# Rounded products for the projections of latent attention, and part of the output product moved into the last decoding sequence

## The chip, the cores and the metric

The kernel runs on one core of one Trainium2 chip. The time is the device time of one execution in microseconds (us). TensorE (PE) multiplies out of the on-chip memory into eight PSUM banks; VectorE (DVE) and ScalarE (ACT) empty these banks and prepare operands; GpSimd (POOL) does elementwise work; SyncE (SP) issues the transfers. The engines run side by side and wait for each other on semaphores.

## The reference, cut to what matters

Two layers of a decoder: the first mixes tokens by multi-head latent attention, the second by a recurrence (RWKV-7); each is followed by a feed-forward part (FFN). The change touches the first layer's attention alone. T = 1072 tokens: 16 meta tokens, 1024 of the prompt, and 8 sequences that are being decoded with 4 tokens each, which look back on 2048 cached tokens in pages of 128.

```python
a = h @ w_qkv_a
c_q = rmsnorm(a[..., :Q_LORA], q_a_norm)                    # 384 wide
c_kv = rmsnorm(a[..., Q_LORA:Q_LORA + KV_LORA], kv_a_norm)  # 256 wide
k_pe = rope(a[..., Q_LORA + KV_LORA:], pos)                 # 64 wide
q = (c_q @ w_q_b).reshape(B, T, 8, 128 + 64)
w_uk = w_kv_b.reshape(256, 8, 128 + 128)[..., :128]
...
hp = hp + o @ w_o      # o: attention output of all 8 heads, 1024 wide
hs = hs + o_sample @ w_o
```

## The kernel before

Everything is float32 and lies transposed: features on the 128 partitions, tokens along the row, in three pieces of 384, 384 and 304 tokens (`PIECES`). PE writes two rings of four PSUM banks: ring A is emptied by ACT, ring V by DVE. `Fill.bank` waits until the bank four fills ago was drained. A matmul on float32 operands is recorded as two instructions. A "rounded" value x_hi is x converted to the type fp32r by ACT; x_lo = x - x_hi is made by DVE (or POOL), rounded as well, and a product is then w_hi x_hi + w_hi x_lo + w_lo x_hi, three matmuls of one instruction each. The attention scores and the FFN are made so already (`product3`, L1018, in the FFN); the latents and the heads' projections are plain float32.

Order of the attention: the latents c_q (`cq`), c_kv (`ckv`) and the rotated key are made and normed (to 142 us). A barrier of all engines (`meet`) follows. Then a loop over four pairs of heads (three turns and the last apart, `two_heads`). In each head there are ten blocks of 104 queries (NQ = 10): PE computes the scores of block n, DVE copies them and takes their maxima (`maxima`), ACT takes the exponentials, DVE scales them (`scaled`), and PE transposes the probabilities two steps later (`turn_probs`, to ring A) and multiplies the values. In between, PE makes value rows for steps n = 0, 2, 3 (`value_rows`, ring A). Three further steps, n = 10 to 12, make what comes next: in the first head of a pair the projections of the second (`project(1, p)`: 3 terms for the queries, 2 for the keys, for each piece p), in the second head the raw rotated queries of the next pair (`raw_queries`, 3 terms for each piece), their rotation on DVE (`take_raw_queries`, `rotated`), and the projections of the next pair's first head. ACT rounds them to `q_hi` and `k_hi` (`round_projected`), DVE makes `q_lo` and `k_lo` (`split_projected`), POOL and DVE the same for the rotated part.

The weights of a pair are loaded by SP (`load_pair`: three transfers of w_q_b, one of w_kv_b). Each engine works through its program in order, and so does SP: for i = 1, 2, 3 it runs `gather((i - 1) * 32, 32)`, a loop that looks up 32 pages and issues two transfers for each into `past_scratch`, then waits for `wkv_used` to reach i (PE signals it in step 3 of the second head), then issues `load_pair(i)`. PE waits for these weights at `raw_queries`, in step 10 of the second head.

The decoding sequences follow, one step of 14.1 us each, n = 0 to 8, of which the last (n = 8) has only the back half of sequence 7: the maxima, transposed probabilities, values, and `fold`. Eight products by the value weights follow, a barrier, and the product by w_o (`out_product_0`): four quarters of 268 tokens, 8 output tiles each, 8 heads as terms, added by DVE to the hidden state `hT` (`add_hidden`). The FFN follows, whose weights SP loads after that barrier.

Of the kernel before, what the change touches and what calls it, by code (L numbers as in the profile page):

```python
# [18 lines left out]
P = 128  # L19
# [79 lines left out]

HEADS_AT = {"q_hi": 31328, "q_lo": 31328 + T, "k_hi": 31328 + 2 * T, "k_lo": 31328 + 3 * T, "k2_hi": 37696, "k2_lo": 37696 + T}  # L100
# [116 lines left out]
def program(nc, A, O):  # L217
    ctx = ExitStack()
    with ctx:
# [52 lines left out]
        q2 = [exact(f"q2_{hh}", hh * T, T) for hh in range(2)]  # L272
        with ExitStack() as place:
# [42 lines left out]
        oT = m(KT, T)  # L316
        cq = m(3, T)
        ckv = m(2, T)
        kraw = m(T)
        kfull = m(T)  # L320
        qlat = m(3, DB, H * DS)
        wqp = m(512)[:, 0:384].rearrange("p (k n) -> p k n", k=3)
# [6 lines left out]
        n2(NQ, KVL + ROPE)  # L329
# [9 lines left out]
        wq = m2(3, 384)  # L339
        wkv = m2(2, 512)  # L340
# [157 lines left out]

        def mixtab(rows, at, n):
            return mix_early[0:rows, at:at + n] if at < NEARLY else mix_late[0:rows, at - NEARLY:at - NEARLY + n]  # L500
# [55 lines left out]
        wq_s, wq_used, wkv_used = sem("w_q_loaded"), sem("w_q_used"), sem("w_kv_used")  # L556
# [4 lines left out]
        gather_s = sem("pages_gathered")  # L561
        wv_s, wo_s, narrow_s = sem("w_v_loaded"), sem("w_o_loaded"), sem("narrow_waits")
# [79 lines left out]
        def _(pe):  # L642
# [4 lines left out]
            wq_t, wkv_t, prob_t = Tally(wq_s), Tally(wkv_used), Tally(prob_s)  # L647
# [149 lines left out]
            def project(hh, p, when):  # L797
                at, w = PIECES[p]
                product(rv, lambda j: wq[:, j, hh * 192:hh * 192 + NOPE], lambda j: cq[:, j, at:at + w], 3, w=w)
                product(rv, lambda j: wkv[:, j, hh * 256:hh * 256 + NOPE], lambda j: ckv[:, j, at:at + w], 2, w=w)  # L800
                mark["projected"][when, hh, p] = rv.filled.n

            def two_heads(last):
                when = "last" if last else "loop"
                for hh in range(2):
# [3 lines left out]
                    ra.done(ins)  # L809

                    def value_rows(t0, n):
                        b = ra.bank()
                        for t in range(n):
                            for k in range(2):
                                ins = mm(b[0:QT, t * VH:(t + 1) * VH], ckv[:, k, (t0 + t) * QT:(t0 + t + 1) * QT],
                                         wkv[:, k, hh * 256 + NOPE:(hh + 1) * 256], k == 0, k == 1)
                        ra.done(ins)

                    def sample_queries():
# [7 lines left out]
                        if hh == 1:  # L827
                            wkv_t.add(pe.drain())
# [38 lines left out]
                    for n in range(NQ + 3):  # L867
# [4 lines left out]
                        elif not last:  # L872
                            if n == NQ:
                                raw_queries()
# [16 lines left out]
            raw_queries()  # L891
            rotated(0)
            for p in range(3):
                project(0, p, "first")
            split_t = [Tally(turned_s), Tally(second_s)]
            with pe.Fori(0, H // 2 - 1) as i:
# [5 lines left out]
                wq_t.enter(i, 64)  # L902
# [7 lines left out]
                wq_t.leave(H // 2 - 1)  # L910
# [3131 lines left out]
```

## Time and profile before

| | before |
|---|---|
| median of 3 runs | 3307.88 us (3303.43 to 3308.81) |
| profiled execution | 3305.95 us, its span 3304.1 us |
| busy: PE, PEld (weight loads), DVE, ACT, POOL | 96%, 87%, 56%, 40%, 36% of the span |
| latents, to the barrier | 142 us |
| four pairs of heads | 142 to 535 us, 98 to 100 us from pair to pair |
| decoding sequences and value products | 535 to 669 us |
| output product, four quarters | from 669 us |

A profile gives for each engine which instructions ran when, and what ended the idle time before them. PE's matmuls are pipelined, so the time between the starts of like ones counts, not the duration of one. "PEclk" is TensorE's granted clock as a share of full speed: 1.00 is 2.4 GHz, 0.50 is 1.2 GHz.

### The profile page before, as it was taken

What the parts mean: (1) busy time and instruction counts of PE and PEld (TensorE: products, weight loads), DVE (VectorE), ACT (ScalarE), POOL (GpSimd) and SP (SyncE); (2) the same over time, 40 slices, a digit from 0 to 9 for tenths busy, and PEclk for the clock granted to TensorE, in tenths of its full rate; (3) what the DMA queues carried; (4) which work ended last, traced back from release to release, by engine and by line L of the source; (5) the groups of instructions that cost most, each with busy time, mean ns of one, the idle gap of its engine ahead of it and who ended that gap; (6) DMA issues with size and microseconds to landing.
All of it is one profiled execution on the core that took longest, in us unless ns stands there. A gap on an engine that the chain in (4) does not pass through costs nothing.

```text
span 3304.1 us, 69890 instructions
## 1 busy us (share of the span) xinstructions
PE 3176.3 (96%) x25744; PEld 2883.2 (87%) x25744; DVE 1840.6 (56%) x3139; ACT 1333.0 (40%) x2785; POOL 1204.4 (36%) x841
## 2 busy tenths in 40 slices
PE   8999999999999999999999999999999999999998
PEld 6688887687999999997999887877788899999998
DVE  3466663216544478757303377777734644457885
ACT  2244445512444533322213365566521354443332
POOL 0000000010766777731222222223213276677771
PEclk9999999999999999999999999999989999999999
DMA  3122224500444544432213201110152155454442
GB/s 112 43 79 66 69 74 147 179 13 20 151 157 157 184 133 142 133 109 69 90 53 114 99 14 34 33 40 27 31 170 51 46 164 157 157 184 141 140 141 77
DMA packets 306260, 330.39 MB, mean 100 GB/s; under 512 B 54350, under 2 KB 287745, under 8 KB 305954
## 3 DMA queue, kind: packets, MB, share of 16 engines
q1 hardware_dynamic: 300178, 308.64, 29.4%
q0 software_dynamic: 5904, 19.21, 1.8%
q8 instruction: 132, 2.16, 0.3%
q14 instruction: 46, 0.38, 0.0%
HBM read 232.05 MB, written 116.16 MB: 105 GB/s over the span
## 4 chain that ended last, share of the span: by engine, by line
PE 71%; DVE 8%; issue 6%; POOL 5%; PEld 3%; ACT 3%; SPq 2%; DMA 1%; DVEq 0%; POOLq 0%; PEldq 0%; ACTq 0%
PE bank L650 67%; PE bank L658 4%; PEld bank L650 3%; POOL wloA L2066 2%; POOL arena L2066 2%; DVE arena L3579 1%; SPq L1753 1%; DVE hT L3650 1%; POOL wloS L2066 1%; POOL table L2066 1%; SPq L1694 0%; SPq L1748 0%; DVE arena L3039 0%; DVE fb L3284 0%; DVE arena L3596 0%
## 5 line engine op out<-in xcount | busy, mean ns | idle before, releaser
L650 PE MATMUL bank<-arena 128*32 128x128 f32 (+18 forms) x7390 | 949.5, 317 | 37.5 <-DVE hT L3650 12.9
L650 PEld LDWEIGHTS bank<-arena 128*128 128x128 f32 (+9 forms) x7390 | 737.1, 166 | 223.0 <-issue 37.5
L2283 ACT COPY arena<-bank 128x512 f32<-128x512 f32 (+14 forms) x527 | 235.0, 484 | 627.8 <-PE bank L650 427.9
L2066 POOL TENSOR_TENSOR arena<-arena 128x512 f32<-128x512 f32 x120 | 164.9, 1374 | 605.0 <-PE bank L650 376.6
L2506 ACT ACTIVATE whiS<-arena 128x512 fp32r<-128x512 f32 x180 | 112.9, 627 | 406.8 <-POOL arena L2066 391.1
L2066 POOL TENSOR_TENSOR wloA<-arena,whiA 128x512 fp32r<-128x512 f32 x180 | 261.6, 1469 | 13.2 <-ACT whiA L2503 13.2
L2066 POOL TENSOR_TENSOR wloS<-arena,whiS 128x512 fp32r<-128x512 f32 x180 | 239.6, 1345 | 49.1 <-ACT whiS L2506 49.1
L3445 DVE TENSOR_TENSOR hT<-hT,bank 128x536 f32<-128x536 f32 x280 | 197.4, 706 | 80.6 <-PE bank L650 80.1
L658 PE MATMUL bank<-table,arena 128*128 128x128 f32 (+5 forms) x1422 | 181.4, 269 | 29.6 <-DVE arena L3159 13.1
L650 PE MATMUL bank<-hiT,whiS 128*128 128x268 f32 x768 | 199.2, 288 | 6.5 <-DVE loT L3284 3.7
L3289 DVE TENSOR_TENSOR arena<-std,bank 128x268 f32<-128x268 f32 x192 | 80.3, 431 | 219.2 <-PE bank L650 207.6
L658 PEld LDWEIGHTS bank<-table,arena 128*128 128x128 f32 (+5 forms) x1422 | 146.5, 135 | 55.4 <-issue 40.7
L3051 DVE TENSOR_TENSOR hT<-hT,bank 128x268 f32<-128x268 f32 (+2 forms) x112 | 52.2, 472 | 221.6 <-PE bank L650 221.1
L2059 POOL TENSOR_TENSOR q<-arena,q 64x1072 fp32r<-64x1072 f32 x4 | 9.8, 2461 | 440.8 <-ACT q L2371 440.8
L3386 DVE TENSOR_TENSOR arena<-arena 128x268 f32<-128x268 f32 x224 | 139.4, 662 | 41.4 <-ACT arena L2544 39.5
L650 PEld LDWEIGHTS bank<-hiT,whiS 128*128 128x128 f32 x768 | 145.7, 190 | 7.6 <-DVE loT L3284 4.4
L3530 DVE SCALAR_TENSOR_TENSOR x_mix<-arena,prm 128x384 f32<-128x384 f32 (+1 forms) x72 | 45.5, 704 | 169.3 <-PEq L1148 169.0
L2136 POOL TENSOR_TENSOR w_lo<-arena,w_hi 128x2048 fp32r<-128x2048 f32 x12 | 56.8, 4736 | 215.7 <-ACT w_hi L2681 215.7
L650 PE MATMUL bank<-hi,whiA 128*128 128x268 f32 x512 | 132.2, 287 | 3.3 <-DVE fb L3284 3.3
L650 PE MATMUL bank<-loT,whiS 128*128 128x268 f32 x512 | 132.2, 287 | 0.0
L650 PE MATMUL bank<-fb,whiS 128*128 128x268 f32 x512 | 131.8, 287 | 0.0
L650 PE MATMUL bank<-fb,whiA 128*128 128x268 f32 x512 | 131.6, 286 | 0.0
(320 smaller groups left out, 8533.1 us busy)
## 6 DMA issues: line engine op xcount, KB each, us to landing
u_scratch<-arena SPq DMA_DIRECT2D x480, 134.0 KB, 1.9
arena<-in_ffn_w_up SPq DMA_DIRECT2D x64, 512.0 KB, 4.1
arena<-u_scratch SPq DMA_DIRECT2D x56, 536.0 KB, 5.1
arena<-in_ffn_w_down SPq DMA_DIRECT2D x112, 256.0 KB, 4.2
arena<-u_scratch SPq DMA_DIRECT2D x56, 402.0 KB, 5.8
arena<-past_scratch SPq DMA_DIRECT2D x32, 640.0 KB, 7.0
past_scratch<-in_cache_kv_latent SPq DMA_DIRECT2D x128, 128.0 KB, 2.4
past_scratch<-in_cache_k_rope SPq DMA_DIRECT2D x128, 32.0 KB, 2.2
```

What stands on the lines that cost most here:

```text
L650: return pe.matmul(out, lhsT, rhs, start=first, stop=last, skip_group_check=group)
L658: return pe.transpose(out, src, ident[0:rows, 0:rows])
L1753: sp.dma_start(dst, src).then_inc(gather_s, 16)
L2066: return pool.tensor_tensor(out, a, b, op)
L2136: pool.tensor_tensor(w_lo[par][:, :, :], w_raw[par][:, :, :], w_hi[par][:, :, :].bitcast(F32), ALU.subtract).then_inc(wlo_s, 1)
L2283: lane.do(act.copy(dst, b if view is None else view(b)), ring.drained)
L2506: ins = act.activation(hi[name][:, :, :], s2t if name == "S2" else lo32[name], ACT.Copy)
L3051: lane.do(dve.tensor_tensor(hT[:, k, at:at + w], hT[:, k, at:at + w], b[:, 0:w], ALU.add), ring.drained)
L3289: dve.tensor_tensor(out, to, (BV, BA)[s][CHAIN[i]][:, 0:TS], ALU.add).then_inc(to_dve_b[layer].sem, 1)
L3386: dve.tensor_tensor(f.us[q, s], f.us[a, s], f.us[b, s], op).then_inc(diff_b[layer].sem, 1)
L3445: ins = dve.tensor_tensor(to[i], to[i], made, ALU.add)
L3530: ins = dve.scalar_tensor_tensor(out=x_mix[:, k, at:at + w], in0=DX[:, k, at:at + w], scalar=prm[:, k, R_MU + row:R_MU + row + 1], in1=nT[ ...
```

## The change

Two parts. First, the projections of the heads (`raw_queries`, `project`) become three rounded products. For that c_q, c_kv and the weights of each pair are rounded by ACT and split by DVE; the rounded latents lie where the hidden state lies, which is stored to memory early and loaded back in four quarters. The weights go to two raw places by turns of which the second serves pairs 1 to 3; PE's signal `wkv_used` for a pair moves from step 3 of its second head to the start of that head, the value weights are copied aside, and ACT rounds the next pair's weights in step 1 of the second head, after a wait for their load. Second, the product by w_o of the first quarter of tokens is cut in two: its first three heads (`three_heads`, two output tiles at a time) are computed in step n = 8 of the decoding sequences, and added by DVE there; after the barrier only heads 3 to 7 are left for that quarter.

```diff
# PE
+            def projection(w_hi, w_lo, x_hi, x_lo, n, w):
+                b = rv.bank()
+                for k in range(n):
+                    mm(b[:, 0:w], w_hi(k), x_hi(k), k == 0, False)
+                    mm(b[:, 0:w], w_hi(k), x_lo(k), False, False)
+                for k in range(n):
+                    ins = mm(b[:, 0:w], w_lo(k), x_hi(k), False, k == n - 1)
+                rv.done(ins)
-            def raw_queries():
-                wq_t.expect(64)
-                pe.wait_ge(wq_s, wq_t.value())
-                for at, w in PIECES:
-                    product(rv, lambda j: wqp[:, j, :], lambda j: cq[:, j, at:at + w], 3, w=w)
+            def raw_queries(*split):
+                for (at, w), n in zip(PIECES, split):
+                    lo_t.expect(n)
+                    pe.wait_ge(lo_s, lo_t.value())
+                    projection(...)
             def project(hh, p, when):
-                product(rv, lambda j: wq[...], lambda j: cq[:, j, at:at + w], 3, w=w)
-                product(rv, lambda j: wkv[...], lambda j: ckv[:, j, at:at + w], 2, w=w)
+                projection(..., 3, w)
+                projection(..., 2, w)
             def two_heads(last):
                     ra.done(ins)
+                    if hh == 1:
+                        wkv_t.add(pe.drain())
...
-                        if hh == 1:
+                        if last and hh == 1:
                             wkv_t.add(pe.drain())
...
+            def three_heads(ks):
+                for k in ks:
+                    product(rv, lambda j: wo[0][:, j, k * P:(k + 1) * P], lambda j: oT[:, j, 0:TS], 3, w=TS)
             for n in range(DB + 1):
                 if back:
                     spread_maxima(n - 1)
+                if not front:
+                    pe.wait_ge(wo_first, wo_first_at + 16)
+                    three_heads((0, 1))
...
                     probs_at = turn_probs(n - 1)
+                if not front:
+                    three_heads((2, 3))
...
+                if not front:
+                    three_heads((4, 5))
                 if back:
                     fold(n - 1, values_at)
+                if not front:
+                    three_heads((6, 7))
# SP
+            sp.wait_ge(a_drained, 10)
+            sp.wait_ge(v_drained, 10)
+            sp.dma_start(h_d[:, :], hx[:, :]).then_inc(early_put, 16)
...
             for i in range(1, H // 2):
                 gather((i - 1) * 32, 32)
                 sp.wait_ge(wkv_used, i)
+                if i == 1:
+                    sp.wait_ge(out_s, out_t.n)
                 load_pair(i)
...
+            sp.wait_ge(early_put, 16)
+            load_hidden(0)
             for half in range(2):
                 sp.wait_ge(page_used, DB - 2 + half)
-                load(wo[half], w[:, 3 * half:3 + 5 * half, :], wo_t)
+                if half == 0:
+                    sp.dma_start(wo[0], w[:, 0:3, :]).then_inc(wo_first, 16)
+                else:
+                    load(wo[1], w[:, 3:8, :], wo_t)
+            for q in (1, 2, 3):
+                load_hidden(q)
# POOL
-                pool.wait_ge(round_s, 14 * pair + 2)
+                pool.wait_ge(round_s, 18 * pair + 12)
# ACT, latents
+            act.wait_ge(early_put, 16)
+            for at, w in PIECES:
+                rounded(ckv_hi[:, :, at:at + w], ckv[:, :, at:at + w])
             for t in range(NQ + 1):
+                if t == 4:
+                    act.wait_ge(wq_s, wq_t.value())
+                    rounded(wqp_hi[:, :, :], raw_qp[0])
                 take(ctok[...])
+            round_cq(1)
             meet(act, here)
+            round_cq(2)
+            rounded(wkn_hi, kv_part(wkv, 0))
+            round_wq(0)
+            act.copy(w_value, kv_part(wkv, 1))
# ACT, two_heads, ahead of the exponential of step n
+                        if hh == 1 and not last and n == 1:
+                            wq_t.expect(64)
+                            act.wait_ge(wq_s, wq_t.value())
+                            rounded(wqp_hi[:, :, :], raw_qp[1])
+                            round_wq(1)
+                            rounded(wkn_hi, kv_part(wkv, 0))
+                        if hh == 1 and not last and n == 4:
+                            act.copy(w_value, kv_part(wkv, 1))
# DVE, two_heads, behind scaled(n - 1)
+                        if hh == 1 and not last and n == 3:
+                            split_wqp(1)
+                            split_wq(1)
+                            rounded()
+                            rest(wkn_lo[:, :, :], kv_part(wkv, 0), wkn_hi)
# DVE, decoding sequences
                     maxima(n - 1)
+                if n == DB:
+                    dve.wait_ge(hidden_back[0][0], hidden_back[0][1] + 16)
+                    for k in range(4):
+                        add_hidden(k, 0, TS)
+                    lane.settle()
+                if n > 0:
                     values_out(n - 1)
+            for k in range(4, KT):
+                add_hidden(k, 0, TS)
```

## Rows read from the trace of the kernel before

**Rows 1.** Busy time by engine, granted clock and DMA in one pair's stretch
```profile
core 0: us, PE busy (x) PEld busy (x) DVE busy (x) ACT busy (x) POOL busy (x), PEclk, DMA share, GB/s
258.00:356.00 98.00, 94.28 (x605) 81.83 (x604) 64.57 (x164) 43.20 (x105) 2.46 (x1) 1.00 0.25 72
```
**Rows 2.** Waits of PE, 140 to 670 us: waiting, for whom, total, times, longest
```profile
PE bank L650 <- DMA arena<-in_mla_w_kv_b: 1.5, 1, 1.5
```
**Rows 3.** Timeline of SP's queue: start, duration, line, transfer
```profile
152.19 0.74 SPq L1753 DMA_DIRECT2D past_scratch<-in_cache_kv_latent  x1
...
232.64 0.52 SPq L1753 DMA_DIRECT2D past_scratch<-in_cache_k_rope  x1
...
234.90 0.49 SPq L1694 DMA_DIRECT2D arena<-in_mla_w_kv_b  x1
236.47 0.56 SPq L1753 DMA_DIRECT2D past_scratch<-in_cache_kv_latent  x1
...
326.13 1.45 SPq L1694 DMA_DIRECT2D arena<-in_mla_w_q_b  x3
```
**Rows 4.** Chain of work that ended last: start, duration, what
```profile
234.90 5.10 DMA arena<-in_mla_w_kv_b
```
**Rows 5.** Timeline of PE: float32 matmuls of the latents (two instructions each)
```profile
101.91 15.64 PE L650 MATMUL bank<-arena 128*128 128x384 f32 x48
...
119.33 12.44 PE L650 MATMUL bank<-arena 128*128 128x304 f32 x48
```
**Rows 6.** Timeline of PE: rounded products of the FFN, starts of two of twelve
```profile
1442.74 0.34 PE L650 MATMUL bank<-u_hi,dn_hi 128*128 128x384 f32 x1
...
1444.84 0.33 PE L650 MATMUL bank<-u_hi,dn_hi 128*128 128x384 f32 x1
```
**Rows 7.** Timeline of DVE, end of the first pair
```profile
246.34 1.27 DVE L3075 TENSOR_TENSOR arena<-arena 128x1072 f32<-128x1072 f32 x1
...
259.38 0.47 DVE L3123 TENSOR_TENSOR k_lo<-bank,k_hi 128x304 fp32r<-128x304 f32 x1 [0.55 <-ACT k_hi L2364]
```
**Rows 8.** Timeline of ACT: latents, then the first pair's second head
```profile
118.10 1.16 ACT L2308 ACTIVATE arena<-arena 128x1152 f32<-128x1152 f32 x1
...
135.69 5.83 ACT L2283 COPY arena<-bank 104x320 f32<-104x320 f32 x11
...
212.05 0.19 ACT L2403 ACTIVATION_READ_ACCUMULATOR arena<-arena 104x1 f32 x1
214.55 1.08 ACT L2403 ACTIVATE arena<-arena 104x936 f32<-104x936 f32 x1 [2.31 <-DVE arena L3149]
```
**Rows 9.** Timeline of DVE, step 4 of the same head
```profile
221.12 0.59 DVE L3144 COPY arena<-bank 104x416 f32<-104x416 f32 x1 [2.52 <-PE bank L650]
```
**Rows 10.** Timeline of PE, same head: transposes at its start, value rows of step 3
```profile
205.97 0.38 PE L658 MATMUL bank<-table,arena 128*128 128x128 f32 x2
...
216.96 1.03 PE L650 MATMUL bank<-arena 128*104 128x128 f32 x8
```
**Rows 11.** Stages as in rows 1, around an idle stretch of PE later in the kernel
```profile
1515.00:1519.00 4.00, 0.90 (x3) 0.19 (x1) 4.00 (x5) 0.00 (x0) 2.32 (x1) 1.00 0.04 13
1519.00:1523.00 4.00, 3.51 (x7) 2.35 (x8) 4.00 (x4) 0.00 (x0) 0.00 (x0) 0.59 0.00 0
```
**Rows 12.** Timeline of DVE: one of the adds of the output product
```profile
682.12 0.43 DVE L3051 TENSOR_TENSOR hT<-hT,bank 128x268 f32<-128x268 f32 x1 [3.18 <-PE bank L650]
```
**Rows 13.** Timeline of PE, last decoding sequence: transposed probabilities, values, fold
```profile
653.73 1.28 PE L658 MATMUL bank<-table,arena 128*128 128x128 f32 x5 [1.59 <-ACT arena L2446]
655.58 4.37 PE L650 MATMUL bank<-arena 128*32 128x256 f32 x34 [0.58 <-ACT arena L2283]
...
661.23 0.63 PE L650 MATMUL bank<-table,arena 128*128 128x32 f32 x4 [0.97 <-DVE arena L3239]
```
**Rows 14.** Stages as in rows 1, the two stretches at the lower clock
```profile
652.70:659.60 6.90, 5.29 (x39) 2.35 (x39) 0.00 (x0) 1.62 (x6) 0.00 (x0) 0.51 0.62 252
...
663.00:673.20 10.20, 9.87 (x37) 8.75 (x37) 1.37 (x8) 0.47 (x1) 0.42 (x1) 0.50 0.32 102
```
**Rows 15.** Stage as in rows 1, where the early store of the hidden state would run
```profile
38.00:100.00 62.00, 62.00 (x204) 38.52 (x203) 16.11 (x28) 6.33 (x10) 0.00 (x0) 1.00 0.00 1
```

More of the change, by code:

```diff
@@ L328, in program @@
         n2 = Carve()
-        n2(NQ, KVL + ROPE)
+        n2(2 * T)
+        wkv = n2(2, 512)
+        n2(NQ * (KVL + ROPE) - n2.at)
+        raw = [Carve(c.at + first * T) for first in (3, 6)]
+        raw_q, raw_qp = [t(3, 384) for t in raw], [t(3, P) for t in raw]
+        assert all(t.at <= c.at + first * T for t, first in zip(raw, (5, 8)))
         ctok_new = n2(KVL + ROPE)
@@ L889, in two_heads @@
                             turn_probs(n - 2)
-            raw_queries()
+            raw_queries(6, 1, 1)
             rotated(0)
+            lo_t.expect(3)
+            pe.wait_ge(lo_s, lo_t.value())
             for p in range(3):
@@ L909, in _ @@
                 prob_t.leave(H // 2 - 1)
[L910 removed]
+                lo_t.leave(H // 2 - 1)
                 wkv_t.leave(H // 2 - 1)
@@ L2319, in take_queries @@
                     take(cq[:, k, at:at + w], P, w)
+                    if k == 0 and behind_first is not None:
+                        behind_first()
                 lane.settle()
@@ L2349, in _, with rounded, round_wq, round_cq @@
             deviations_of(3, 0)
-            take_queries(2)
+            def rounded(dst, src):
+                act.activation(dst, src, ACT.Copy).then_inc(round_s, 1)
+            def round_wq(place):
+                rounded(wq_hi_01[:, :, :], raw_q[place][:, 0:2, :])
+                rounded(wq_hi_2, raw_q[place][:, 2, :])
+            def round_cq(p):
+                at, w = PIECES[p]
+                act.wait_ge(norm_s, 7 + p)
+                rounded(cq_hi[:, :, at:at + w], cq[:, :, at:at + w])
+            act.wait_ge(early_put, 16)
+            for at, w in PIECES:
+                rounded(ckv_hi[:, :, at:at + w], ckv[:, :, at:at + w])
+            take_queries(2, lambda: round_cq(0))
             deviations_of(3, 1)
@@ L3096, in _, with rest, rounded, split_wqp @@
             norm(ckv, ckv, 2, R_KVN, mark["norm_kv"])
+            round_t, lo_t = Tally(round_s), Tally(lo_s)
+            def rest(out, raw, hi):
+                return lane.do(dve.tensor_tensor(out, raw, hi.bitcast(F32), ALU.subtract), lo_t)
+            def rounded():
+                round_t.expect()
+                dve.wait_ge(round_s, round_t.value())
+            def split_wqp(place):
+                rounded()
+                rest(wqp_lo_01[:, :, :], raw_qp[place][:, 0:2, :], wqp_hi[:, 0:2, :])
+                rest(wqp_lo_2[:, :], raw_qp[place][:, 2, :], wqp_hi[:, 2, :])
+            def split_wq(place):
+                rounded()
+                rest(wq_lo[:, 0:2, :], raw_q[place][:, 0:2, :], wq_hi_01[:, :, :])
+                rounded()
+                rest(wq_lo[:, 2, :], raw_q[place][:, 2, :], wq_hi_2)
+            def split_cq(p):
+                at, w = PIECES[p]
+                rounded()
+                rest(cq_lo[:, :, at:at + w], cq[:, :, at:at + w], cq_hi[:, :, at:at + w])
             for p in range(3):
                 norm_piece(cq, cq, 3, R_QN, Tally(a_drained, mark["norm_q"][p]), *PIECES[p])
+                if p == 0:
+                    for at, w in PIECES:
+                        rounded()
+                        rest(ckv_lo[:, :, at:at + w], ckv[:, :, at:at + w], ckv_hi[:, :, at:at + w])
+                    split_cq(0)
             meet(dve, here)
@@ L3184, in two_heads @@
                                  lambda b: b.rearrange("p (a w) -> p a w", a=1))
+            split_wqp(0)
+            split_cq(1)
+            split_cq(2)
             take_raw_queries()
+            rounded()
+            rest(wkn_lo[:, :, :], kv_part(wkv, 0), wkn_hi)
+            split_wq(0)
             rotated(0)
@@ L3204, in _ @@
                 round_t.leave(H // 2 - 1)
+                lo_t.leave(H // 2 - 1)
             two_heads(H // 2 - 1, True)
@@ L3254, in adds @@
                     s, l = QUARTERS[q]
+                    if layer == 0 and ks[0] == 0:
+                        dve.wait_ge(hidden_back[q][0], hidden_back[q][1] + 16)
                     for k in ks:
```

72 lines of the change are left out of this document (54 added, 18 removed).

## The prediction

> **What bounds the kernel now.** I read the table by stages first. In the loop over the pairs of heads the matrix engine is busy 94.3 of 98 us [rows 1]: PE bounds it, and a microsecond taken from its matmuls counts, if nobody else is late in its place. The waits of PE say who nearly is. One of them, 1.5 us and once only, is for the weights of the next pair of heads [rows 2]. It deserves a look, since the change touches just these loads. SP gathers the pages of the cache between them, 32 pages to a pair, and that loop is slow: its first transfer is issued at 152.19, its last at 232.64, 2.53 us a page. Only then come the four loads of pair 1, the last issued at 234.90 [rows 3] and landed 5.10 us later, at 240.0 [rows 4]. So **before the change SP is just in time**: the weights land 1.5 us after PE wants them, at the end of the pair's second head.
>
> **Part one, the projections.** Removed per pair: 3 float32 terms of the raw rotated queries and 2 x (3 + 2) of the heads, 13 in all, each over token pieces of 384, 384 and 304. A term of 384 costs PE 15.64 / 24 = 0.652 us (each is recorded as two instructions), one of 304 12.44 / 24 = 0.518 us [rows 5]. In their place come three rounded matmuls a term. The same kind exists in this kernel: twelve of 384 start 2.10 us before the next twelve [rows 6], 0.175 us each, and by the columns 0.14 us for 304. Saved: 0.652 - 0.525 = 0.127 us and 0.518 - 0.42 = 0.098 us, so 13 x (0.127 + 0.127 + 0.098) = 4.6 us a pair; I take 4.4, 18 us for four pairs.
>
> Not all of it is kept. At the end of a pair's first head nothing but PE's products orders the work, so the whole of 5 terms counts, 1.7 us. At the end of the second the chain runs raw queries, DVE's rotation, ACT's rounding, DVE's splits, and DVE waits for PE and ACT only before the last k_lo, 0.55 us [rows 7]. There the shorter raw product counts (1.0 us) and only 0.55 of the 1.7 us: 1.55 us.
>
> Added on ACT and DVE, at the start of the second head: ACT rounds 384 + 768 + 384 + 512 columns of weights, and DVE makes their rest, 2048 columns in five instructions. At ACT's 1.16 us for 1152 columns [rows 8] that is 2.2 to 2.4 us; at DVE's 1.27 us for 1072 [rows 7] it is 2.6 us. DVE sat idle 2.52 us just there [rows 9]: hidden, up to some tenths; uncovered it would be 2.6 us a pair. The copy of the value weights (0.6 us) stands in step 4, where no row of mine shows ACT pressed; I take nothing, at most 0.6.
>
> **The wait that is added** is the heart of it. `act.wait_ge(wq_s, ...)` stands in step n == 1 of the second head, ahead of the second exponential. In the first pair it wants the loads of pair 1, and SP issues those behind the same 32 pages as before: their order is not changed. The signal that frees the weights comes earlier, but in the first pair SP isn't waiting for it, it is gathering. ACT is through the first exponential at 212.24 and starts the second at 214.55 [rows 8]; the weights land at 240.0 [rows 4]. SP itself starts later, too. ACT's eleven copies of the latents end at 141.5 now, 0.53 us each [rows 8]. The new wait ahead of the fifth (the first weights land there at about 138.4), 0.5 us of rounding, seven copies and 1.16 us for a piece of cq end them at 143.8: the barrier and the gather are 2 us later. So the weights land at 242, the rounding ends at 244.3, and the second exponential is 29.7 us late. Queued behind ACT's wait are all its exponentials and the copies that drain PE's ring A. PE can fill three more banks; then its value rows of step 3, before at 216.96 [rows 10], need a bank that ACT emptied 0.75 us earlier. DVE waits for the exponential too. **PE is held for 29 us, once**, and since this hangs on SP's clock, the 4 us saved before it in this pair are lost in it.
>
> Later pairs: from the transposes that start a second head (205.97) [rows 10] to the end of ACT's first exponential are 6.3 us; a load issued right behind the transposes lands after some 0.3 + 1.5 + 5.1 = 6.9 us. That is 0.6 us of waiting and 2.3 of rounding, against 2.31 us that ACT idled there anyway [rows 8]: 0.3 to 0.5 us a pair with DVE. SP's second gather ran slower, 2.8 us a page (236.47 to 326) [rows 3]; shifted by 2 us it ends at 328, while the second head of that pair starts, by the pairs' 100 us and a shift of 27, at 332: just in time.
>
> After the stall the clock costs something as well. Behind a stretch in which PE was busy 0.9 of 4 us the granted clock fell to half, 1.2 instead of 2.4 GHz (0.59 over the next 4 us) [rows 11], and PE's work there takes twice as long. I put 2.5 us, between 0 and 4.
>
> **Part two, the output product.** The first quarter's first three heads are 24 float32 matmuls of 268 columns. Eight take 3.18 + 0.43 = 3.61 us from one of DVE's adds to the next [rows 12], so 10.8 us move from behind the last barrier into the last sequence. PE idles there 1.59, 0.58 and 0.97 us [rows 13] and a few tenths before the value product: 3.4 us are filled. That is what the places are worth at one clock. But the clock is half from 652.7 to 659.6 and from 663 to 673.2, with PE busy 5.3 and 9.9 us of these [rows 14]; half of that, 7.6 us, is lost to it. So the part gains 3.4 us at the least and 11 if the filled gaps keep the clock up. In the second stretch it stayed low with PE busy, on matmuls of 32 columns at first, and those remain. I take 8.5 us, nearer to the upper end, since the first fall came with the gaps.
>
> Here a rule of the Trainium skill would say more than the rows: TensorE: Matmul & The Clock Gate, section "Why this matters for your kernels", puts drops in the middle of a kernel down to idle gaps of PE between bursts. By that rule filled gaps leave no reason for either fall and the whole 11 us come back, which would put the sum 2.5 us lower. The trace agrees for the first fall and speaks against it in the second.
>
> What this part brings along: the hidden state is stored early and its four quarters (1.1 MB each) are loaded back. The store runs after 38 us, where the DMA moved 1 GB/s while PE was busy throughout [rows 15]: hidden, and if that cover were gone, up to 20 us. The quarters queue on SP around the loads of w_o: the first ahead of them, the others behind them and ahead of the FFN's first weights, which aren't wanted before four quarters of 8 x 3.61 us have gone by. DVE's adds for the quarter, 0.43 us each [rows 12], lie beside the moved matmuls; its values of the last sequence wait for four of them, hidden by the next two products. I count nothing, and 3 us if SP holds up the barrier.
>
> **The sum**, against the profiled execution (3305.95 us, span 3304.1): +29 stall, +2.5 clock, -1.5 old wait for the weights, -3 x 1.55 ends of pairs, -3 x 1.7 ends of first heads, +1.0 later waits, -8.5 part two: +12.75 us. The median of the runs shown is 1.9 us above the profiled one; from the middle between them, 3306.9, I get about **3319 us**.
>
> **Rivals.** *Slower gather:* the first loop runs at the second's 2.8 us a page instead of 2.53; nothing before says why one was slower, and new code ahead of it may shift it. 32 x 0.28 = 9 us more, 3328 us; chance 0.14. *Rounding buys nothing:* if three rounded matmuls with three weight loads cost what one float32 term does, 10 us of savings go: 3329 us. Against it: rows 6 show their spacing with their loads. 0.04. *The savings are whole:* part two gives 11 us, the pairs keep 4.4 us each after the anchor (13.3 instead of 9.8), the clock after the stall costs nothing: 29 - 1.5 - 13.3 - 11 + 1 = +4 us, 3311 us, no difference that can be told; 0.16. *Faster:* the stall stays below the savings after it. These are at most 26 us, so for 6.6 us of gain the stall must be 19 us, and the weights of pair 1 must land 10 us before 242: a gather loop of 2.2 us a page or less. Neither loop of the trace was below 2.5. At 2.0 us a page the stall is 12 us and the kernel at 3294 to 3303 us; 0.06. *Forecast:* 0.60.
>
> **Range and chances.** A measurement of this kernel tells about 0.2%, 6.6 us, from no change. The bounds of the forecast are a stall of 26 to 31 us, a clock cost of 0 to 4, 8 to 14 us in the pairs and 3.4 to 11 in part two: 3308 to 3331 us; whole savings with a short stall and the slower gather reach a little further. I give 3307 to 3332. Faster 0.06, same 0.2 (whole savings and the low end of the forecast), slower 0.74.
>
> **What would show it.** In the profile after: one wait of ACT, and with it of PE, from about 213 to 242 us, ended by the load of mla_w_kv_b, and a granted clock of 0.5 behind it; products of five terms in 2.6 instead of 3.3 us; later pairs of 95 instead of 98.3 us; the last sequence without its gaps. The forecast is wrong if SP issues the loads of pair 1 well before 233 us, or if ACT's second head doesn't wait for them.

## The result

| | before | after |
|---|---|---|
| median | 3305.81 us (3303.43 to 3308.81, 7 runs) | 3315.42 us (3311.11 to 3318.67, 7 runs) |
| profiled span | 3304.1 us | 3309.3 us |

The ratio is 1.0027, 95% interval 1.0017 to 1.0036: slower by 9.6 us. The forecast was 3319 with 3307 to 3332 as its range. The profiled execution of the changed kernel was the shortest of its seven, and the one with the highest mean granted clock (0.989; the other six 0.985 to 0.988), so its span tells less of the loss than the medians do.

The page of the changed kernel shows the loss at once. First the two lines for PE and its clock, the span in 40 slices of 83 us:

```profile
PE   8979999999999999999999998999999899999998
...
PEclk9989999999999999999999999999999999999999
```

The third slice, 166 to 248 us, is the one in which PE was less busy. The table of waits of the same kernel, from 130 to 700 us (who, for whom, total, times, longest), names the cause:

```profile
POOL q L2136 <- ACT q L2476: 459.0, 4, 156.5
...
ACT wqp_hi L2431 <- DMA arena<-in_mla_w_kv_b: 23.8, 2, 23.0
PE bank L676 <- ACT arena L2360: 23.4, 4, 21.8
```

ACT stood once for 23 us before the rounding of the next pair's weights (L2431), until the load of `in_mla_w_kv_b` had landed, and PE once for 21.8 us until ACT emptied a bank of its ring (L2360). (POOL's wait above them is idle time of an engine with little to do here.) Before the change the same load cost PE 1.5 us [rows 2].

The timeline of ACT shows what stands around that wait (start, duration, line, operation; in brackets the idle time before it and what ended it):

```profile
214.81 1.17 ACT L2516 ACTIVATE arena<-arena 104x1040 f32<-104x1040 f32 x1
215.88 0.19 ACT L2516 ACTIVATION_READ_ACCUMULATOR arena<-arena 104x1 f32 x1
239.03 0.52 ACT L2431 ACTIVATE wqp_hi<-arena 128x384 fp32r<-128x384 f32 x1 [22.96 <-DMA arena<-in_mla_w_kv_b]
239.46 0.83 ACT L2431 ACTIVATE wq_hi<-arena 128x768 fp32r<-128x768 f32 x1
240.19 1.02 ACT L2431 ACTIVATE x_hi<-arena 128x384 fp32r<-128x384 f32 x2
241.12 1.06 ACT L2516 ACTIVATE arena<-arena 104x936 f32<-104x936 f32 x1
```

The timeline of PE shows what it held:

```profile
209.13 0.38 PE L684 MATMUL bank<-table,arena 128*128 128x128 f32 x2
...
220.69 0.26 PE L676 MATMUL bank<-k_lo,q 128*104 128x208 f32 x1
242.79 2.04 PE L676 MATMUL bank<-arena 128*104 128x128 f32 x8 [21.84 <-ACT arena L2360]
```

The second exponential starts at 241.12 instead of 214.55 [rows 8], and the value rows of step 3 at 242.79 instead of 216.96 [rows 10], 25.8 us late. SP's queue says why the load came so late (its transfers of one page start 2.53 us apart, as before):

```profile
227.99 0.54 SPq L1814 DMA_DIRECT2D past_scratch<-in_cache_kv_latent  x1
...
230.51 0.54 SPq L1814 DMA_DIRECT2D past_scratch<-in_cache_kv_latent  x1
231.31 0.52 SPq L1814 DMA_DIRECT2D past_scratch<-in_cache_k_rope  x1
232.10 1.48 SPq L1751 DMA_DIRECT2D arena<-in_mla_w_q_b  x3
233.63 0.49 SPq L1751 DMA_DIRECT2D arena<-in_mla_w_kv_b  x1
```

The weights are asked for at 233.63, behind the 32nd page, as they were at 234.90 [rows 3]; what changed is that ACT wants them in the middle of the head and not PE at its end. The stages from there on (busy time of each engine, then PEclk, the DMA's share and GB/s):

```profile
222.00:236.00 14.00, 0.00 (x0) 0.00 (x0) 0.00 (x0) 0.00 (x0) 0.00 (x0) 0.54 0.35 104
...
240.00:244.00 4.00, 1.21 (x6) 1.21 (x7) 1.59 (x6) 4.00 (x11) 0.00 (x0) 0.50 0.28 79
244.00:248.00 4.00, 4.00 (x22) 4.00 (x22) 3.06 (x8) 1.49 (x7) 0.00 (x0) 0.50 0.17 47
248.00:252.00 4.00, 4.00 (x17) 3.56 (x17) 1.47 (x4) 0.94 (x4) 0.00 (x0) 0.70 0.25 75
285.00:379.60 94.60, 90.77 (x648) 86.62 (x647) 67.28 (x169) 45.65 (x110) 2.51 (x1) 1.00 0.25 71
```

For 14 us no engine computes, and PE comes back at 1.2 GHz, until about 250.4. The last row is an undisturbed pair: 94.3 us from pair to pair (by POOL's one instruction of each pair, 279.91, 374.20 and 468.45) against 98.3 before. PE has more instructions in it than before [rows 1], and is done sooner.

Where the time went, from a landmark in one trace to the same in the other:

| landmark | before | after | later by |
|---|---|---|---|
| pair 0, transposes of the first head | 159.43 | 161.74 | 2.3 |
| of the second head | 205.97 | 209.13 | 3.2 |
| value rows of its step 3 | 216.96 | 242.79 | 25.8 |
| pair 1, first head | 260.69 | 285.30 | 24.6 |
| pair 1, second head | 305.97 | 329.07 | 23.1 |
| pair 2, first head | 358.95 | 379.58 | 20.6 |
| pair 2, second head | 404.24 | 423.37 | 19.1 |
| pair 3, first head | 457.22 | 473.84 | 16.6 |
| pair 3, second head | 502.23 | 517.13 | 14.9 |
| last sequence, maxima spread | 651.75 | 667.11 | 15.4 |
| first add of the second quarter | 703.80 | 711.84 | 8.0 |
| end of the span | 3304.1 | 3309.3 | 5.2 |

Of the 25.8 us, 22.6 arise in the 34 us from 209 to 243, and the heads after that give back 10.9. The last 2.8 us lie behind the changed code: from 711 us to the end the clock stood at half for about 33 us before and for about 28 us in this trace.

The clock has a hand in the first rows as well. Between 15 and 25 us, in unchanged code, its mean was 0.69 before and 0.83 after, and the transposes of the latents begin 1.26 us sooner (133.82 against 135.08). At the barrier PE then waits 2.31 us instead of 1.24 and works at half clock for 6.8 us behind it, where it had full clock before: the heads start 2.3 us later.

### The profile page after: what moved, and what is told of

Read it like the earlier page. It is cut to its first block, busy times and chain, and to the rows that moved or that the text cites. A ratio compares the mean times of both kernels' runs of the same rounds, so it can differ in the third digit from the quotient of the medians.

```text
span 3309.3 us, 70294 instructions
## 1 busy us (share of the span) xinstructions
PE 3160.4 (96%) x25900; PEld 2901.1 (88%) x25900; DVE 1864.7 (56%) x3173; ACT 1347.3 (41%) x2811; POOL 1202.6 (36%) x841
## 4 chain that ended last, share of the span: by engine, by line
PE 71%; DVE 9%; PEld 6%; issue 4%; POOL 4%; ACT 2%; SPq 2%; DMA 1%; DVEq 0%; PEldq 0%; ACTq 0%; POOLq 0%
PE bank L676 68%; PEld bank L676 6%; PE bank L684 4%; POOL wloA L2143 1%; DVE arena L3745 1%; SPq L1814 1%; DVE hT L3816 1%; POOL arena L2143 1%; POOL wloS L2143 1%; DVE x_mix L3696 0%; SPq L1751 0%; SPq L1809 0%; DVE arena L3290 0%; DVE arena L3762 0%; DVE arena L3154 0%
## 5 line engine op out<-in xcount | busy, mean ns | idle before, releaser
L676 PE MATMUL bank<-arena 128*128 128x268 f32 (+19 forms) x7078 | 849.6, 309 | 55.8 <-ACT arena L2360 25.9
L676 PEld LDWEIGHTS bank<-arena 128*128 128x128 f32 (+10 forms) x7078 | 674.7, 164 | 206.6 <-issue 34.9
L2360 ACT COPY arena<-bank 128x512 f32<-128x512 f32 (+14 forms) x527 | 234.3, 484 | 629.0 <-PE bank L676 431.4
L684 PE MATMUL bank<-table,arena 128*128 128x128 f32 (+5 forms) x1422 | 181.0, 269 | 27.3 <-DVE arena L3302 13.1
## 6 DMA issues: line engine op xcount, KB each, us to landing
hT<-hidden_scratch SPq DMA_DIRECT2D x5, 1072.0 KB, 13.2
```

Source lines behind the costliest of these rows:

```text
L676: return pe.matmul(out, lhsT, rhs, start=first, stop=last, skip_group_check=group)
L684: return pe.transpose(out, src, ident[0:rows, 0:rows])
L2360: lane.do(act.copy(dst, b if view is None else view(b)), ring.drained)
```

## The experiments

The theory was: the stall hangs on the number of pages that SP gathers ahead of the next pair's weights, everything else of the change gains, and each part is worth what its own stage shows.

**Dose of the stall.** The gather's 128 pages are spread over the four pairs; three kernels cut them in another way, and so move the load of pair 1's weights on SP's queue by 10 or 5 pages forward, or 5 back. Nothing else is touched.

```diff
# g22 (g27: 27, 32, 32, 37; g37: 37, 32, 32, 27)
-                gather((i - 1) * 32, 32)
+                gather((0, 22, 54)[i - 1], (22, 32, 32)[i - 1])
...
-            gather(96, 32)
+            gather(86, 42)
```

> The changed kernel with 22 instead of 32 pages gathered ahead of the loads of pair 1 (32 and 32 ahead of the next two, 42 behind the last). Theory one (PE's stall hangs on SP's gather): SP is at the loads some 25 us earlier, at about 207, has to wait for the start of the second head at 209, and the weights land at 216 or 217, where ACT wants them at 216. PE's wait of 21.8 us shrinks to about 1, and the half clock behind it (about 3.5 us of PE's time) goes too: 25 us faster than the changed kernel, about 3290 us, and 0.5% faster than the kernel before. Theory two (the loss is in what the rounding adds: ACT's and DVE's splits, PE's weight loads, the clock after the barrier; the wait would be paid elsewhere anyway): within 3 us of the changed kernel, about 3313 us.

> As the last, with 27 pages first (27, 32, 32, 37). Theory one: 5 pages of 2.53 us are 12.7 us, the weights land at 226 and PE waits 9 us: 12 to 13 us faster than the changed kernel, about 3303 us, with a half clock still behind the wait. Theory two: as the changed kernel, 3313 to 3316 us.

> The other way, with 37 pages first (37, 32, 32, 27). Theory one: 12.7 us more, PE waits 34 us and the kernel takes about 3328 us; the later loads of the weights come no later than their heads. Theory two: as the changed kernel.

| pages ahead of pair 1's weights | median | ratio to before | ACT's longest wait for them |
|---|---|---|---|
| 22 | 3291.74 us | 0.9956 (0.9943 to 0.9970) | 0.5 us in the first pair |
| 27 | 3304.09 us | 0.9996 (0.9987 to 1.0005) | 13.4 us |
| 32, the change | 3315.42 us | 1.0027 (1.0017 to 1.0036) | 23.0 us |
| 37 | 3327.46 us | 1.0064 (1.0049 to 1.0079) | 36.1 us |

Five pages cost 12.4, 11.3 and 12.0 us: 2.4 us a page, the time in which SP gets through one (2.53). The wait goes with it, from the table of waits of g27:

```profile
ACT wqp_hi L2431 <- DMA arena<-in_mla_w_kv_b: 13.8, 2, 13.4
```

And from that of g37:

```profile
ACT wqp_hi L2431 <- DMA arena<-in_mla_w_kv_b: 36.6, 3, 36.1
```

At 22 pages it is all but gone; the timeline of SP in g22 has the load issued 20.9 us sooner (not 25, since SP is through with its pages before the second head starts at 210.79, and waits for that):

```profile
212.78 0.49 SPq L1751 DMA_DIRECT2D arena<-in_mla_w_kv_b  x1
```

In the timeline of its ACT the rounding waits 0.46 us:

```profile
217.55 0.19 ACT L2516 ACTIVATION_READ_ACCUMULATOR arena<-arena 104x1 f32 x1
218.20 0.53 ACT L2431 ACTIVATE wqp_hi<-arena 128x384 fp32r<-128x384 f32 x1 [0.46 <-DMA arena<-in_mla_w_kv_b]
```

So the cause is shown, and g22 is a version that beats both kernels: 13 us faster than before, with the arithmetic of the changed kernel.

The Trainium skill, page DMA: Bandwidth & Descriptors, section "Rules for kernel authors", says that spreading transfers over several issuing engines gives no bandwidth and only saves the issuing sequencers' time. Here just that time was short: in the 14 idle microseconds the DMA engines were busy at 0.35 and moved 104 GB/s, while one sequencer worked through its list. Issuing the weights from another engine was not tried; that it would do what taking ten pages away did is not shown.

**Would the other cut have helped before the change?**

```diff
# before_g22: the kernel before, with the same cut
-                gather((i - 1) * 32, 32)
+                gather((0, 22, 54)[i - 1], (22, 32, 32)[i - 1])
```

> The kernel before with 22, 32, 32 and 42 pages: its only wait for the weights of a pair, 1.5 us, goes, or comes back at another pair if SP isn't through with 32 pages there. 1 to 1.5 us faster, 3304 us, which the rounds can hardly tell from no change; the trace shows the wait. It says that the gain of moving the loads forward is the changed kernel's own and not the page loop's.

3304.4 us (3300.5 to 3311.1), ratio 1.0000 (0.9991 to 1.0010). PE's 1.5 us for these weights [rows 2] are gone from its waits, and the time is the same to within the interval's 3 us. Ten pages more in the last pair, 42 in all, cost nothing that it shows. The cut's 24 us in the changed kernel are therefore the stall, and at most 3 us anything of its own.

**The parts alone, with and without the stall.** part_two is the kernel before plus `three_heads` in the last sequence; part_one is the changed kernel without it; part_one_g22 is part_one with the cut of g22.

```diff
# part_one and part_one_g22: the changed kernel without the moved heads
-                if not front:
-                    three_heads((2, 3))
...
-                first = 3 if at == 0 else 0
+                first = 0
```

> The kernel before with the second part of the change alone: three heads of the output product's first quarter in the last decoding sequence (the hidden state stays on chip, so nothing is stored or loaded for it). If the gain of that part is the filled gaps and one of two falls of the clock, as the trace of the changed kernel has it (the last sequence to the first add of the second quarter 7.3 us shorter), it is 7 us faster than the kernel before, about 3299 us. If the clock falls twice as before: 3.4 us, 3302 us. If both falls go: 11 us, 3295 us.

> The changed kernel with its second part undone: all eight heads of the first quarter's output product behind the last barrier, DVE's adds with them; the hidden state is still stored early and loaded back. If the two parts add up, this is the changed kernel's 3315 us plus the 7 to 8 us that the second part alone was worth on the kernel before: 3323 us. If the second part owes its gain to what the first one leaves (a later start, loads that land sooner by comparison), it is 3315 to 3318 us.

> The same with 22 pages ahead of the loads of pair 1, so the rounded products without their stall. By the steps of the trace (the second to fourth pair together 12 us shorter than before, the start of the first 2 to 3 us longer, the wait for the first weights gone): 6 to 8 us faster than the kernel before, about 3298 us. If the rounding really costs what it saves, as theory two had it: 3305 us.

| | median | ratio to before | against before |
|---|---|---|---|
| part_two | 3296.82 us | 0.9976 (0.9967 to 0.9985) | -8.2 |
| part_one | 3325.67 us | 1.0059 (1.0046 to 1.0073) | +20.3 |
| part_one_g22 | 3297.33 us | 0.9978 (0.9967 to 0.9989) | -8.1 |
| both, with the stall | 3315.42 us | 1.0027 (1.0017 to 1.0036) | +9.6 |
| both, without (g22) | 3291.74 us | 0.9956 (0.9943 to 0.9970) | -13.3 |

The parts are independent to within about 3 us: 20.3 - 8.2 = 12.1 against 9.6, and -8.1 - 8.2 = -16.3 against -13.3. The remainders have opposite signs, which speaks against an interaction of the two. In the traces some 2 us of each are there before part two begins: POOL's first instruction, at the start of the pairs, comes at 160.52 in part_one and 158.46 in the changed kernel, at 158.22 in part_one_g22 and 160.17 in g22. The code up to there is the same in all four; the clock is not. Between 134 and 156 us it stood at half for 10.2 us in the two late ones, and for 6.8 and 3.4 us in the other two, and 3.4 us more at half clock cost up to 1.7 us (an estimate: half of the stretch). With one trace of each this is a difference between executions as much as between programs.

**Are the moved heads in the right place?** In the last sequence PE still waits 1.17 us for DVE's spread maxima, and the granted clock falls behind it. g22_ahead puts the first two of the moved output tiles ahead of `spread_maxima`, and DVE's adds for them with them.

```diff
# g22_ahead, against g22
-                if back:
-                    spread_maxima(n - 1)
                 if not front:
                     pe.wait_ge(wo_first, wo_first_at + 16)
                     three_heads((0, 1))
+                if back:
+                    spread_maxima(n - 1)
```

> The kernel with 22 pages first (3291.7 us), and in the last decoding sequence the first two of the moved output tiles ahead of the spreading of the maxima instead of behind it, DVE's two adds for them too. It fills the one gap of 1.17 us that the change left. If that gap is what brings the clock down in this stretch (3.4 to 7 us at the half clock, with PE busy): 1.2 + 1.7 to 3.4 us faster, about 3288 us. If the fall comes from the narrow matmuls ahead of the gap, it stays and 1 us is gained, 3290.5 us. If DVE's adds ahead of the maxima hold up the exponentials: no gain.

3289.05 us (3287.34 to 3292.23), ratio 0.9952 (0.9939 to 0.9966): 2.7 us below g22, which these intervals do not tell apart. The stages of its trace say what the move did not do:

```profile
642.00:646.00 4.00, 2.06 (x13) 1.72 (x12) 1.18 (x4) 1.12 (x4) 0.00 (x0) 1.00 1.01 409
646.00:650.00 4.00, 4.00 (x14) 2.95 (x12) 0.43 (x1) 0.65 (x2) 0.00 (x0) 0.59 1.07 372
...
662.00:666.00 4.00, 3.67 (x19) 3.12 (x19) 0.77 (x4) 0.00 (x0) 0.00 (x0) 0.73 0.20 49
666.00:670.00 4.00, 4.00 (x16) 3.24 (x16) 0.43 (x1) 1.26 (x2) 2.10 (x2) 0.85 0.61 213
```

PE is idle for half of the first stretch (1.94 us of waiting for ACT's exponentials stand there), and both falls are still there, 3.4 us each as in g22. The gap had been moved, not filled.

**Does the barrier's gap cost clock in the first phase?** In the changed kernel PE waits 2.3 us at the barrier at about 140 us, and the queries' raw projection behind it runs at half clock, one product every 0.32 us. g22_busy puts products on constants there, into a bank that nobody reads.

```diff
# g22_busy, against g22_ahead
+            def idle_work(n):
+                b = rv.bank()
+                for _ in range(n):
+                    mm(b[:, 0:384], ones, table[:, 0:384], True, True)
+
+            idle_work(2)
             norm_t.expect(3)
             pe.wait_ge(norm_s, norm_t.n)
             meet(pe, here)
+            idle_work(1)
```

> g22_ahead with three 384-column float32 products on constants more, into a bank that nobody reads yet: two ahead of the barrier in the prologue, one behind it (float32 products of that width take 0.65 us each in the trace). Question: does the granted clock's fall in the prologue (half from 141.4 to 148.1 us in the changed kernel, right behind the gap of 2.3 us at 139.9) come from the gap, and what is it worth. Theory 'the gap makes the fall': the queries' raw projection, 0.32 us a product, goes at 0.175, and the first pair of heads starts 2 to 3 us sooner; 3286 us against the 3289 of g22_ahead. Rival 'something later than TensorE sets the start': the clock stays full and the heads start where they did, 3289. Rival 'the fall comes anyway': half clock as before and the added products cost up to 1 us, 3290.

The stage from 142 to 148 us, of g22_ahead:

```profile
142.00:148.00 6.00, 5.14 (x16) 5.17 (x17) 3.47 (x5) 3.21 (x6) 0.00 (x0) 0.50 0.46 117
```

The same stage of g22_busy:

```profile
142.00:148.00 6.00, 5.43 (x31) 4.92 (x31) 4.43 (x6) 2.47 (x5) 0.00 (x0) 1.00 0.59 151
```

With three useless products the clock stays at 2.4 GHz, and PE gets through 31 instructions in place of 16. The pairs start at 158.91 instead of 162.27, 3.4 us sooner; 0.95 of it was there when the raw projection began (141.91 against 142.86), 2.4 came from the clock. So another engine does not set the start, and the full clock is worth what the theory said.

That the gap makes the fall is only in part shown. All eight traces of the changed kernel and its variants without the added products have a fall there, of 3.4 to 10.2 us, and the one trace with them has none. But in four of the eight (g22, g37, part_one, g22_two_of_three) it begins at 138 to 140 us, ahead of the barrier's gap, in or behind a wait of 0.3 to 1.05 us for ACT among the transposes of the latents. An example is g22, by the timeline of PE (the same nine transposes take 1.65 us in g22_ahead):

```profile
139.21 2.54 PE L684 MATMUL bank<-table,arena 128*104 128x128 f32 x9 [0.33 <-ACT arena L2360]
144.06 0.66 PE L676 MATMUL bank<-x_hi,wqp_hi 128*128 128x384 f32 x1 [2.31 <-DVE wqp_lo L3215]
```

The stage around it:

```profile
136.00:142.00 6.00, 5.41 (x25) 2.52 (x24) 5.36 (x8) 3.78 (x11) 0.00 (x0) 0.77 0.18 62
```

And behind the shorter gap of 1.24 us the kernel before kept its clock, where before_g22 and part_two, with the same code there, had 3.4 us at half. What brings the fall now and not then is open.

The whole kernel took 3287.38 us (3285.44 to 3290.61), ratio 0.9943 (0.9931 to 0.9956), 1.7 us below g22_ahead and not told apart from it. At the last add of the output product 1.6 of the 3.4 us were left (781.65 against 783.23): the falls in the last sequence came at other places and held longer, a mean granted clock of 0.89 against 0.92 from 641 to 686 us. Against before it is the fastest complete version, by 17.8 us.

**How much of a pair is PE's?** g22_two_of_three leaves out the third product of each projection, the low part of the weights times the high part of the tokens.

```diff
# g22_two_of_three, against g22
                     mm(b[:, 0:w], w_hi(k), x_hi(k), k == 0, False)
-                    mm(b[:, 0:w], w_hi(k), x_lo(k), False, False)
-                for k in range(n):
-                    ins = mm(b[:, 0:w], w_lo(k), x_hi(k), False, k == n - 1)
+                    ins = mm(b[:, 0:w], w_hi(k), x_lo(k), False, k == n - 1)
```

> g22 (the changed kernel with pages cut 22, 32, 32, 42) without the third product of every projection of heads: the low part of the weights times the high part of the tokens is left out, so this part of the computation is missing and the numbers are coarser. It asks how much of the first phase is bound by TensorE after the change. Thirteen terms of a pair lose one rounded product each, 0.14 to 0.175 us: 13 x 0.17 = 2.2 us a pair, 9 us over four pairs. Theory 'TensorE sets the length of a pair': 3291.7 - 9 = 3283 us. Rival 'ScalarE's and VectorE's chain of splits and maxima sets it, and the three products ride beside it': within 2 us of 3291.7.

3278.51 us (3274.14 to 3282.7), ratio 0.9922 (0.9905 to 0.994), 13.2 us below g22. The expectation's sum was wrong: it took each of the 13 terms once, though each goes over three token pieces, so that 13 x (0.175 + 0.175 + 0.142) = 6.4 us a pair leave PE, and not 2.2. By the traces the later pairs fell from 94.3 us to 90.6 and 90.3, 3.7 and 4.0 of the 6.4. PE's waits from 260 to 560 us, with the ends of two second heads among them, show who took over; g22 has none of the two there:

```profile
PE bank L676 <- DVE q_lo L3264: 2.6, 2, 1.3
...
PE bank L676 <- DVE k_lo L3264: 1.3, 2, 0.7
```

(2.6 + 1.3) / 2 = 1.95 us of waiting a pair, at the splits that end a second head. With three products PE's own work sets the ends of the heads; with two it is DVE's chain. PE's work is not the whole pair even so: in the changed kernel as in the one before it waits 3.4 us of each pair, in four waits of up to 1.2 us, for DVE's scaling of the probabilities (13.1 us in 16 waits over the four pairs, in both), which no run here took away. The first theory holds at the ends of the heads, and of the next saving of this kind on PE about six tenths would be kept.

## Why the prediction was right, and where it was off

**The wait that is added: right, 3.2 us too large.** The bet was that `act.wait_ge(wq_s, ...)` moves the need for pair 1's weights to a point where SP, still gathering, cannot serve it, and that everything on ACT's queue and PE's ring stands behind it. Place, chain and length (29 forecast, 25.8 found) came out. The excess sits in the start of the gather: the barrier was put 2 us later for the rounding on ACT among the latents' copies, and the weights' landing with it at 242. ACT's new work found idle time there (its copies of the latents end at 140.3): from the first transpose of the latents to the load of the page table it is 7.6 us (133.82 to 141.43) against 7.05 before (135.08 to 142.13), 0.6 later and not 2. The other part is none of the change's doing: these transposes began 1.26 us sooner in this trace, by the clock at 15 to 25 us, and SP needed 0.6 us less from that load to the weights. So the weights are issued at 233.63 and not at 237, and the rounding begins at 239.03. The 2.3 us of rounding were 2.1.

**The clock after the stall: right in kind.** Half clock until about 250.4, with some 8 us of PE's work at it. From the value rows to pair 1 the lag fell by 1.2 us, where the forecast, with +2.5 for the clock, -1.5 for the old wait and -1.55 for the head's end, had 0.55; with the 2.5 us that such an end gained later (below), the clock cost some 2.8.

**First heads: right.** Forecast 1.7 us each; found 1.5, 1.5 and 1.7. In pair 0, whose savings the forecast gave up to the stall, the first head became 0.85 us longer: PE waits 2.00 us for DVE's k_lo at its start (1.05 before), and the clock is at half for 3.4 us behind that wait. g22 has both as well, so this much is left in the faster kernel.

**Second heads: mis-sized.** Forecast 1.55 us less 0.5 for later waits; found 2.5 in pair 1 and in pair 2. The step that failed is "only 0.55 of the 1.7 us" counts, since DVE waits for PE and ACT only before the last k_lo [rows 7]. The end of a second head in the changed kernel, from the timeline of DVE:

```profile
272.63 1.27 DVE L3190 TENSOR_TENSOR arena<-arena 128x1072 f32<-128x1072 f32 x1
...
284.90 0.46 DVE L3266 TENSOR_TENSOR k_lo<-bank,k_hi 128x304 fp32r<-128x304 f32 x1
```

And PE's first instruction of the next head:

```profile
285.30 0.39 PE L684 MATMUL bank<-table,arena 128*128 128x128 f32 x2
```

From the rotation's first instruction to DVE's last k_lo it was 259.85 - 246.34 = 13.5 us and is 285.36 - 272.63 = 12.7; its wait of 0.55 us is gone. But the next head's transposes stood at 260.69, 0.84 us behind that k_lo: PE's own queue, not DVE, was last. From the rotation to the transposes it was 14.35 us and is 12.67, 1.68 less, so the whole 1.7 us of the five terms counted, with the raw projection's 1.0 in front of it. The row of DVE alone had been read as the end of the chain; PE's next row beside it would have shown that it was not. The 0.3 to 0.5 us for later waits were not found: ACT's second wait for these weights, 0.8 us, stands ahead of the barrier and not in a later pair.

**Part two: right in size, wrong in its reason.** 7.4 us in the trace, 8.2 alone in part_two, 8.5 forecast. The forecast let the first fall of the clock go, with the gaps, and the second stay. It was the other way round in the trace of the changed kernel, first by the timeline of PE:

```profile
665.31 0.63 PE L676 MATMUL bank<-table,arena 128*128 128x32 f32 x4
667.11 0.59 PE L676 MATMUL bank<-arena,table 128*128 128x4 f32 x2 [1.17 <-DVE arena L3378]
667.55 5.71 PE L676 MATMUL bank<-arena 128*128 128x268 f32 x12
673.05 1.05 PE L684 MATMUL bank<-table,arena 128*128 128x128 f32 x5
674.03 5.38 PE L676 MATMUL bank<-arena 128*128 128x268 f32 x46
```

and by its stages:

```profile
667.00:674.00 7.00, 6.89 (x19) 5.27 (x19) 1.23 (x5) 1.12 (x4) 0.00 (x0) 0.52 1.03 401
674.00:681.00 7.00, 6.89 (x54) 4.59 (x54) 1.68 (x5) 0.65 (x2) 0.00 (x0) 1.00 1.13 353
```

The moved products fill the gaps for the probabilities (1.59, 0.58 and 0.97 us [rows 13] are gone), but the first of them stand behind a wait of 1.17 us and run at half clock; the second stretch at half clock [rows 14] is not there. That it is not was the luck of this trace: in g22, g27, g37 and part_two a second fall, of 3.4 or 6.8 us, stands around the last barrier. What holds over all traces is the sum. Without part two the clock is at half for 17.1 us in this stage in before and part_one_g22 (6.8 and 10.2) and for 20.5 in part_one and before_g22 (6.8 and 13.6); in the eight traces with it, for 6.8 to 10.3. That is 10 us less on average, worth some 5 us (an estimate: half of them), and with the 3.1 us of gaps it makes the 8.2 of part_two.

The rule of the Trainium skill that the prediction weighed, in TensorE: Matmul & The Clock Gate, "Why this matters for your kernels" (drops come from idle gaps between bursts), would as applied there have had no fall left. In the trace a fall of 6.8 us stands with PE busy 6.89 of 7 us, behind a gap of 1.17 us. The page means longer gaps than this one, so the trace speaks against its use here and not against the page; and behind the stall of 21.84 us the clock was at half, as the page has it.

**What it brings along.** The early store and the three returning quarters of the hidden state (10.2 us of issue on SP at 664.35, beside PE's work) held nobody up, as counted.

**The sum.** Forecast +29 - 0.55 - 5.1 - 2.1 - 8.5 = +12.75. Found by the same landmarks +25.8 - 1.2 - 4.7 - 5.0 + 0.5 - 7.4 = +8.0, and +9.6 by the medians (the +0.5 lies between the last second head and the last sequence; no part of the sum had it). The stall was 3.2 too large and the second heads 2.9 too small, both to the same side; part two was 1.1 too large. The trace is of the shortest execution, so that its 8.0 lies near the medians' 9.6 is in part luck; and about 1.3 us of the stall's 3.2 was the clock in another stage. Of the rivals, the slower gather did not come (2.53 us a page again), the rounded products gave what rows 6 had promised, and "faster" failed at the condition it named: its gather of 2.2 us a page. The experiment g22 is that rival brought about by fewer pages instead of faster ones: 32 x 2.2 = 70 us of gather were its condition, 22 x 2.53 = 56 us are g22's.

## What to carry to other kernels

Where a change lets an engine want data earlier, look up on the issuing queue when they are asked for, not when the buffer comes free: a loop of small transfers ahead of them is a fixed delay, and cutting the loop elsewhere may cost nothing. Read the end of a stage on every engine that could be last before taking only a part of a saving. Take away the loss first, then judge the parts: here a change worth 13 us had measured as 10 us slower.

## What the runs showed of the hardware

- With three products on constants around a wait of PE the clock stayed at 2.4 GHz over the next 6 us, in which it was at 1.2 without them (31 instructions instead of 16); one trace with them, eight without.
- The same code had different stretches at half clock from trace to trace: 3.4, 6.8 or 10.2 us between 134 and 156 us, and around the last sequence and the last barrier 6.8 us in the changed kernel, 3.4 and 3.4 in g22, 6.8 and 3.4 in g27, 3.4 and 6.8 in g37. By half of each stretch, an estimate, this is worth up to 3.4 us in the first stage and 1.7 in the second. It goes from execution to execution too: the mean granted clock of the changed kernel's seven ran from 0.985 to 0.989. A landmark in one trace is no better than that.
- A rounded product with its own weight load took 0.175 us at 384 columns in the projections too, from one start to the next; three of them replace a float32 term of 0.652.
